# HGRN queries behind the last merge, unread states and zero products left out, lag-zero row on GpSimd

## What is computed

```python
zero_states = (jnp.zeros((bsz, 2, H_A, DK_A, DV_A)), ...)          # prompt
h, st = _block(h, mod, zero_states, layer_params(l), lower[l], None)
new_gdn.append(st[0]) ...                                          # final states: of the prompt only
z, _ = _block(z, mod, cached, layer_params(l), lower[l], rows)     # sample: final states are dropped

def step(s, xs):                      # HGRN, one chunk (GDN and mLSTM have the same form)
    qd_i, kd_i, v_i, a_i, gl_i = xs
    o = qd_i @ s + a_i @ v_i          # product with the state before the chunk, and within the chunk
    s = s * gl_i[..., None] + jnp.einsum('bhcd,bhce->bhde', kd_i, v_i)

def _hyena_filters(...):              # two-sided filter on a circle; its lag zero stands once
    circ = jnp.concatenate([h[:, :, 0], zero, h[:0:-1, :, 1]], axis=0)
```

## Time and profile before

| what | us |
|---|---|
| median of three runs (1619.14 to 1622.45) | 1622.17 |
| the profiled execution | 1620.4 |
| its span | 1618.6 |
| PE busy, all of the span | 1462.0 |
| DVE busy | 704.8 |
| ACT busy | 403.8 |
| POOL busy | 311.1 |

### The profile page before, as it was taken

The page is one execution under the profiler, slowest core; times in us unless marked ns, Lnnn a source line. Parts: engine busy times, 40 slices in busy tenths (PEclk is TensorE's granted clock), DMA queues, the critical chain, the costliest instruction groups (busy, mean ns, idle before and its releaser), DMA issues. The chain is left out here.

```text
span 1618.6 us, 21858 instructions
## 1 busy us (share of the span) xinstructions
PE 1462.0 (90%) x8308; PEld 1071.9 (66%) x8308; DVE 704.8 (44%) x1290; ACT 403.8 (25%) x775; POOL 311.1 (19%) x452
## 2 busy tenths in 40 slices
PE   5999999996999999798869798879999999999855
PEld 1565885853888898555545553758888888888711
DVE  2605582047566655456656621624222222222246
ACT  2211100132644554312112201241212212121101
POOL 0200000011222111224423412011112121111163
PEclk9999989998999999878978999979999999999988
DMA  9624532100390000100001140029999999999787
GB/s 359 195 79 132 179 106 78 53 1 0 146 412 2 1 2 1 30 10 1 27 33 39 65 165 0 20 89 405 385 391 377 386 382 397 390 392 342 244 302 294
DMA packets 101058, 279.78 MB, mean 173 GB/s; under 512 B 22609, under 2 KB 39251, under 8 KB 99580
## 3 DMA queue, kind: packets, MB, share of 16 engines
q1 hardware_dynamic: 85148, 235.55, 39.3%
q0 software_dynamic: 15840, 43.28, 7.0%
HBM read 230.97 MB, written 64.52 MB: 183 GB/s over the span
## 5 line engine op out<-in xcount | busy, mean ns | idle before, releaser
L2494 PEld LDWEIGHTS PS<-arena 128*128 128x128 f32 x2240 | 259.1, 192 | 43.3 <-ACT arena L2980 23.5
L2494 PE MATMUL PS<-arena 128*128 128x128 f32 x2240 | 263.0, 276 | 5.6 <-DMA arena<-in_exp_w_down 4.3
L690 PE MATMUL PS<-arena 128*128 128x512 f32 x384 | 176.4, 614 | 1.5 <-DVE arena L1140 1.5
L2801 DVE TENSOR_SCALAR arena<-PS,arena 128x1024 f32<-128x1024 f32 x70 | 89.8, 1283 | 141.8 <-PE PS L2502 141.8
L2502 PE MATMUL PS<-arena 128*128 128x512 f32 x280 | 137.8, 615 | 0.9 <-DVE arena L2794 0.8
L690 PEld LDWEIGHTS PS<-arena 128*128 128x128 f32 x384 | 74.2, 198 | 88.5 <-issue 87.7
L2794 DVE TENSOR_TENSOR arena<-arena,PS 128x128 f32<-128x128 f32 x70 | 20.1, 288 | 183.4 <-ACT arena L2986 183.4
L2986 ACT ACTIVATE arena<-PS 128x128 f32<-128x128 f32 x70 | 19.4, 277 | 313.5 <-PE PS L2494 313.5
L702 PE MATMUL PS<-arena 128*128 128x256 f32 (+1 forms) x400 | 89.0, 389 | 0.0
L702 PEld LDWEIGHTS PS<-arena 128*128 128x128 f32 x400 | 77.9, 215 | 10.1
L3073 POOL DMA_INDIRECT arena<-h_rows,arena x70 | 71.7, 1024 | 58.4 <-POOL arena L3070 58.4
(11 more groups left out here) (456 smaller groups left out, 2280.8 us busy)
## 6 DMA issues: line engine op xcount, KB each, us to landing
arena<-in_exp_w_gate SPq DMA_DIRECT2D x70, 512.0 KB, 6.0
arena<-in_exp_w_up SPq DMA_DIRECT2D x70, 512.0 KB, 8.6
arena<-in_exp_w_down SPq DMA_DIRECT2D x70, 512.0 KB, 17.0
y_rows<-arena SPq DMA_DIRECT2D x70, 512.0 KB, 17.1
y_rows<-cst SPq DMA_DIRECT2D x1, 21504.0 KB, 58.2
arena<-in_w_in SPq DMA_DIRECT2D x16, 1024.0 KB, 6.2
arena<-in_w_mod SPq DMA_DIRECT2D x32, 512.0 KB, 3.5
arena<-in_w_mod SPq DMA_DIRECT2D x4, 2048.0 KB, 14.9
```

What stands on the lines that cost most here:

```text
L690: pe.matmul(PS[:, b0, :], w[:, k, i * P:(i + 1) * P], hT[:, k, 0:SMP], start=(k == 0), stop=(k == KT - 1))
L2494: mm = pe.matmul(PS[:, bank, 0:P], w[:, k, :], xT[j % 2][:, k, :], start=k == 0, stop=k == KT - 1)
L2801: dve.tensor_scalar(yb[j].rearrange("p (h n) -> p h n", h=2), PS[:, 4 + 2 * (j % 2):6 + 2 * (j % 2), :], gate_col[j % 2], None, ALU.mult). ...
```

## The change

Three edits.

1. **Order of DVE in HGRN.** Of the eight query products of unit u + 1, levels 0 to 2 stay behind the merge of level 5. Levels 3 to 7 move from behind the merges of levels 5 and 6 to behind `hgrn_merge(u + 1, 0)`, in front of `hgrn_take(u)`.
2. **Work left out.** Pair 0 leaves out every product with its zero first state (L864, L908, L918 and, for units 0 and 1, L1052), and with them `w_turn`, `w_turned_out` and `new_values`. The last pair leaves out its final states: `mlstm_state`, `gdn_state`, their `take` steps on DVE, and `keys_decay` and `mlstm_keys` on POOL. HGRN then starts on the last outputs taken (`g_otaken`, `m_otaken`) in place of the last states taken.
3. **Row of lag zero.** L2558 and L2559 leave DVE. POOL does them in `first_lag`, one add and two multiplies for each of tiles 0 and 4, on a buffer of its own. `filter_spectrum(0)`, `prompt_spectrum` and ACT's squares of tiles 0 and 4 wait for the new semaphore `f_lag`.

```diff
                 def gdn_out(i, x):
-                    pe.wait_ge(g_vn, nth(i, x))
+                    if i > 0:
+                        pe.wait_ge(g_vn, nth(i - 1, x))
+                    else:
+                        pe.wait_ge(g_wt, nth(i, x))
                     pe.wait_ge(g_qd, nth(i, x))
                     for pt in range(2):
-                        pe.matmul(PS[...], gqd[i % 2][x][:, pt, :], gS[:, s, d, pt, :], start=True, stop=False)
+                        if i > 0:
+                            pe.matmul(PS[...], gqd[i % 2][x][:, pt, :], gS[:, s, d, pt, :], start=True, stop=False)
...
-                    w_turn(i, 0)
-                    w_turn(i, 1)
+                    if i > 0:
+                        w_turn(i, 0)
+                        w_turn(i, 1)
...
-                    w_state(i, 0)
-                    w_state(i, 1)
-                    mlstm_state(i, 1)
+                    if i > 0:
+                        w_state(i, 0)
+                        w_state(i, 1)
                     if i + 1 < PAIRS1:
+                        mlstm_state(i, 1)
                         scores(i + 1, 0)
                     gdn_out(i, 0)
-                    gdn_state(i, 0)
                     if i + 1 < PAIRS1:
+                        gdn_state(i, 0)
                         scores(i + 1, 1)
...
                         hgrn_merge(u, r)
                         if u + 1 < HU:
                             if r == 5:
-                                hgrn_queries(u + 1, range(4))
-                            elif r == 6:
-                                hgrn_queries(u + 1, range(4, LV + 1))
+                                hgrn_queries(u + 1, range(3))
...
                     if u + 1 < HU:
                         hgrn_merge(u + 1, 0)
+                        hgrn_queries(u + 1, range(3, LV + 1))
                     hgrn_take(u)
...
                 act.wait_ge(fo_done, 1)
-                act.wait_ge(g_staken, len(UNITS))
-                act.wait_ge(m_staken, len(UNITS))
+                act.wait_ge(g_otaken, len(UNITS))
+                act.wait_ge(m_otaken, len(UNITS))
...
-                    if t in (0, 4):
-                        dve_order.done(i)
-                        dve_order.done(dve.tensor_tensor(row_tmp, hsd[0:1, t, 0], hsd[0:1, t, 1], ALU.add))
-                        i = dve.tensor_scalar(hsd[0:1, t], spread(row_tmp, 1, 2), 0.5, None, ALU.mult)
                     i.then_inc(f_hs, 1)
...
+                def first_lag(t):
+                    pool.wait_ge(f_hs, t + 1)
+                    pool_order.done(pool.tensor_tensor(lag_tmp, hsd[0:1, t, 0], hsd[0:1, t, 1], ALU.add))
+                    for side in range(2):
+                        i = pool.tensor_scalar(hsd[0:1, t, side], lag_tmp, 0.5, None, ALU.mult)
+                    i.then_inc(f_lag, 1)
```

More of the change, by code:

```diff
@@ L332, in trunk_program @@
         PAIRS1 = len(UNITS) // 2
+        KEPT = len(UNITS) - 2
         LAST_N = LV - 1
@@ L863, in mlstm_out @@
                     for pt in range(2):
-                        pe.matmul(PS[:, 4, 130 * pt:130 * pt + 130], mqd[:, pt, :], mS[:, s, d, pt, :], start=True, stop=False)
+                        if i > 0:
+                            pe.matmul(PS[:, 4, 130 * pt:130 * pt + 130], mqd[:, pt, :], mS[:, s, d, pt, :], start=True, stop=False)
                         for par in range(2):
@@ L964, in _ @@
                         elif n == 5:
-                            mlstm_state(i, 0)
+                            if i + 1 < PAIRS1:
+                                mlstm_state(i, 0)
                         else:
@@ L1051, in hgrn_out @@
                     for pt in range(2):
-                        pe.matmul(PS[:, 2, P * pt:P * pt + P], hKQ[u % 2][:, pt, LV, :], hS[:, s, d, pt, :], start=True, stop=False)
+                        if u >= 2:
+                            pe.matmul(PS[:, 2, P * pt:P * pt + P], hKQ[u % 2][:, pt, LV, :], hS[:, s, d, pt, :], start=True, stop=False)
                         for par in range(2):
@@ L1469, in _ @@
                             mlstm_weights(i, 1)
-                        else:
+                        elif i + 1 < PAIRS1:
                             mlstm_take_state(i, 0)
@@ L1478, in _ @@
                         row_minus(i + 1, 1)
-                    new_values(i, 0)
-                    new_values(i, 1)
-                    mlstm_take_state(i, 1)
+                    if i > 0:
+                        new_values(i, 0)
+                        new_values(i, 1)
                     if i + 1 < PAIRS1:
+                        mlstm_take_state(i, 1)
                         first_level(i + 1, 0)
                     take_out(i, 0)
-                    take_state(i, 0)
                     if i + 1 < PAIRS1:
+                        take_state(i, 0)
                         attention(i + 1, 0)
@@ L1489, in _ @@
                     take_out(i, 1)
-                    take_state(i, 1)
                     if i + 1 < PAIRS1:
+                        take_state(i, 1)
                         attention(i + 1, 1)
@@ L1803, in _ @@
                         keys_by_beta_out(i + 1)
-                    w_turned_out(i, 0)
-                    w_turned_out(i, 1)
+                    if i > 0:
+                        w_turned_out(i, 0)
+                        w_turned_out(i, 1)
                     if i + 1 < PAIRS1:
@@ L1946, in _ @@
                         eye(gPm[x], g_pmi)
[L1947 to L1948 removed]
                     if i + 1 < PAIRS1:
                         for x in range(2):
+                            keys_decay(i, x)
+                        for x in range(2):
                             keys_beta(i + 1, x)
[L1952 to L1954 removed]
+                        mlstm_keys(i, 0)
+                        mlstm_keys(i, 1)
                         for x in range(2):
@@ L2026, in trunk_program @@
         ctmp = part(r2_at + 5376, TOK)
-        row_tmp = part(r2_at + 13092, 512)[0:1].rearrange("p (o n) -> p o n", o=2)
+        row_tmp, lag_tmp = (part(r2_at + 13092 + 512 * i, 512)[0:1].rearrange("p (o n) -> p o n", o=2) for i in range(2))
         mid_row = [part(a, MW)[0:1] for a in (r1_at + 6144, r2_at + 8740)]
```

45 lines of the change are left out of this document (23 added, 22 removed).

## The result

The kernel after takes 1611.02 us (median of 8 runs, 1608.47 to 1613.70), the kernel before beside it 1619.16 us (8 runs, 1614.35 to 1622.45). The ratio is 0.995, with a 95% interval of 0.994 to 0.9961: faster by 8.1 us, where 27 were forecast. The sign was right, and 1611 lies outside the range of 1586 to 1603.

A forecast was written before the change was run, and what follows sets the result against it. PE bounds GDN and mLSTM; in HGRN, PE's waits for late DVE merges and the low-clock spells after them. 2.0 + 2.1 + 1.9 + 19.8 + 1.1 = 26.9 us off 1620.4 gave 1593 us, range 1586 to 1603.

The forecast's parts named there:

- The pairs: Ahead of HGRN: pair 0 without its zero state gains 2.0 us, pair 4 without its final states 2.1 us.
- PE's waits for the merges: End of each HGRN unit: both PE waits for DVE gone but for some 0.1 us, hgrn_out 1.93 us earlier.
- The price of the moved queries: HGRN: five query products take 2.3 us on DVE; new wait of about 1.0 us before level 1, unit 13.3 us.
- All five now lie beside POOL (781.65 to 785.03): HGRN, at unit 5: all five moved query products run beside POOL's key products, so they take 2.3 us.
- C: Rival, HGRN: order gives nothing, level 1 still at 786.46, needing 3.2 us for the five queries; 1615 us, chance 0.05.
- D: Rival, HGRN: queries pay nearly four times beside POOL, 4.8 us, level 1 comes 1.6 later; 1630 us, chance 0.03.
- The clock: HGRN units 0 to 7: low-clock spells go but for one (3.1 us); eight distances 19.8 us less.
- The premise that a wait smaller than the 1.64 us of GDN leaves no fall: HGRN: the new 1.0 us wait is smaller than the 1.64 us GDN bears at clock 1.00, so spells go.
- The loop: hgrn_out(0) to hgrn_out(9): eight distances lose 19.8 us, the last 1.1; 124.6 us forecast, 145.5 before.
- The lag row: Tiles 0 and 4: moving it from DVE to POOL gains 0, bounds -0.5 and +2; POOL's operations 2.7 us in all.
- moves along: Stages after HGRN: they hang on it by semaphores alone and shift with it, unchanged in themselves.
- rival A: HGRN: low-clock spells stay, as many as before, elsewhere in the units; 1600 us, chance 0.20.

The follow-up runs named there:

- e2_skips_only: The kernel before with only the left out zero-state products and unread final states: 1612.83 us, ratio 0.9957 to the kernel before.
- e5_filled_pause: The kernel before with four extra matmuls in PE's wait for each unit's last merge, ahead of hgrn_out: 1604.55 us, ratio 0.9907.
- e9_after_filled: The kernel after with extra matmuls in PE's wait ahead of each first level (2 or 3; 7, 8, 13 for units 2, 4, 8): 1610.94 us.
- e12_again: e4_pool_waits unchanged, one more profiled execution: 1597.93 us.
- e6_all_pool_behind: e4_pool_waits with POOL's state-key multiply also waiting for the next unit's queries: 1588.28 us, ratio 0.9814 to the kernel before.
- e4_pool_waits: The kernel after with POOL's norm and w3sd instructions in units 1, 2, 4 and 8 waiting for the next unit's queries: 1599.16 us, ratio 0.9865.
- e7_keys_behind: e4_pool_waits with POOL's key products also waiting for the queries: 1625.17 us, ratio 1.0033 to the kernel before.
- e1_order_only: The kernel before with the new query order alone: 1614.97 us, ratio 0.9956 to the kernel before.
- e13_again: e1_order_only unchanged, one more profiled execution: 1613.0 us.

## Why the prediction was wrong, step by step

- **The pairs**: right, and in both terms. 4.1 us forecast; from pair 0 to the table load 4.1 are gone both in after and in e2_skips_only. In after, 2.1 of them lie between the first `mlstm_out` products of pairs 0 and 1 (2.0 forecast) and 2.0 between those of pair 4 and the table load (2.1 forecast).
- **PE's waits for the merges**: right. They are 0.20 to 0.22 us in most units where 0.41 and 1.62 stood, and 0.59 in the last units.
- **The price of the moved queries**: the term 4 x 0.43 + 0.6 = 2.3 us was mis-sized. It measures 2.36 + 0.41 = 2.77, the new wait 1.36 instead of 1.0, and the unit 13.8 instead of 13.3. The 0.43 was read from three products, beside the start of POOL's keys alone; that one of the moved ones would also meet L2005 wasn't counted. Eight units of 0.5: about 4 us.
- **The step that failed**: "All five now lie beside POOL (781.65 to 785.03)" was read off unit 5 and taken for all units. In units 0, 1, 3 and 7 POOL goes on behind the keys with the norms and w3sd, one instruction of 1.3 to 3.0 us after another, and in the kernel before they began just behind the queries. Moving the queries 1 to 2 us later put them under those. The five products took 2.37 + 2.53 = 4.90 us at the end of unit 3 and 3.65 + 3.09 = 6.74 at the end of unit 7. That is the condition of rivals C and D (over 3.2 us), which I had priced for all units or none, and as a factor on DVE's own time where the rows of the lag row showed a hold to the end of POOL's instruction; it held in three of nine (2.36 + 1.48 = 3.84 in unit 1). The waits cost (2.87 - 1.36) + (3.49 - 1.36) + (5.34 - 1.36) = 7.6 us.
- **The clock**: that the seven spells of before hung on PE's waits and would go was right (e5_filled_pause), the count of what is left was wrong. One low spell was expected in the loop, for 3.1 us; three came in the profiled execution, one at each of those three waits, worth 4.5 us (e9_after_filled). The premise that a wait smaller than the 1.64 us of GDN leaves no fall doesn't hold as a rule: unit 5 of e12_again had one with 1.38.
- **The loop summed up**: eight units at 0.5 are 4.2; 7.6 for the long waits; 4.7 for the clock in them (16.43, 17.55 and 19.84, less 13.83 and the waits' excess); unit 4 has 0.45 (14.28); 1.2 and 3.1 had been set aside for the norms' sums and one spell: 4.2 + 7.6 + 4.7 + 0.45 - 4.3 = 12.6, and 12.7 is what the eight units came out above the forecast 110.7. The ninth came out 0.7 better, which leaves the 12.0. With the cause taken away (e6_all_pool_behind) the loop is 122.4, 2 us better than forecast, and the run 1588.3 for a forecast of 1593. It is another kernel than the forecast's, so it bears out the cause and not the number.
- **The lag row**: 0, right, though POOL's operations took longer than the 2.7 us set down. Timeline, POOL, after, tile 0:

```profile
828.88 1.25 POOL L3025 TENSOR_TENSOR arena<-arena 1x512 f32<-1x512 f32 x1 [13.08 <-DVE arena L2565]
830.22 2.95 POOL L3027 TENSOR_SCALAR arena<-arena 1x512 f32<-1x512 f32 x2
```

  4.2 us for each tile; PE ran on to L2278 (L2268 before) without a gap.
- **Behind HGRN**: "moves along" was too simple. The same instructions lasted 249.3 to 261.1 us in the profiled executions, by where the lower clock fell. The profile after had 4.6 us of that against it. How much of the medians' 18 us miss it makes can't be said from single profiles; that share stays open.
- **The range** had its upper end at 1603, from rival A. A case with a few units each paying the price of C or D was missing; 7.6 and 4.5 us on top of 1593 would have reached 1605, with the query price 1609.

## What to carry to other kernels

When an instruction is moved on an engine that another can hold, look at what the other engine does at the new place in every iteration, not in a typical one: the rare long instruction decides. Here one more wait on POOL, for work that nobody was in a hurry for, was worth 12 us by the medians, more than the change itself. A second one came out 8 to 11 lower still, of which the units show 2.4 as its own. And where TensorE pauses at the same point of each iteration, see the granted clock before the pause is counted at its length: filling 1.6 us in each unit with useless matmuls gave 15 us.

## What the runs showed of the hardware

- A DVE product with both inputs in SBUF that begins under a long POOL instruction ends 0.3 us after it: 0.41 us alone, 2.53 and 3.09 under instructions of 2.36 and 3.01; the one-partition L2558, 0.68 us alone, ended 0.55 after. Against short ones the two take turns (0.22 alone, 0.46 beside products of 0.45). The Trainium skill says as much on another page than the one I had cited: SBUF — State Buffer, section "Who interferes with whom", has a DVE instruction with two SBUF inputs contend with a GpSimd one that reads SBUF, and calls the shared pair of ports "an exclusive lock". The runs agree. By it the price should have been read as the length of POOL's instruction, not as a factor on DVE's. POOL lost little: its seven key products took 3.14 us beside the queries and 3.04 without them. But it is held in its turn when it begins second: at 770.40 in after, L1992 began under L1525 and took 0.59 us, where it takes 0.41 alone (700.49 in e4_pool_waits).
- TensorE's lower clock came, at each of five successive units, with waits of 0.41 and 1.62 us a unit, and not in those units once the longer was filled. A wait of 1.36 us a unit left it at 1.00 in most. With a wait of 2.9 us or more that nothing filled, every unit was below 1.00, all nine of e7_keys_behind (3.04 to 3.55 us) among them. With shorter waits it differed between executions of one kernel: after 2.43 us the unit was at 1.00 in e1_order_only and at 0.90 in e13_again, and one unit of e12_again was at 0.89 with 1.38.
- One kernel's own executions can differ by more than a change is worth: e1_order_only lay between 1603.6 and 1618.1 us over eight runs, while e2_skips_only lay within 2.4 us over five.
